# Latent attention: the first pair's queries and keys ahead of the last chunk of the gates' group

## What is computed

```python
def mla_attention(c_q, c_kv, k_rope, q_a_g, kv_a_g, w_q_b, w_kv_b, cos, sin):
    q = (rmsnorm(c_q, q_a_g) @ w_q_b).reshape(b, s, MLA_HEADS, MLA_QK_DIM)
    q_nope = q[..., :MLA_NOPE_DIM]
    q_rope = rope(q[..., MLA_NOPE_DIM:], cos[:, None, :], sin[:, None, :])
    kv = (rmsnorm(c_kv, kv_a_g) @ w_kv_b).reshape(b, s, MLA_HEADS, MLA_NOPE_DIM + MLA_V_DIM)
    k_nope = kv[..., :MLA_NOPE_DIM]
    v = kv[..., MLA_NOPE_DIM:]
    k_r = rope(k_rope, cos, sin)
    ...
        sc = (jnp.einsum('bqhd,bkhd->bhqk', qn, k_nope)
              + jnp.einsum('bqhd,bkd->bhqk', qr, k_r)).astype(jnp.float32) * scale
        ...
        p = jax.nn.softmax(jnp.where(mask, sc, NEG), axis=-1)
        return jnp.einsum('bhqk,bkhd->bqhd', p.astype(v.dtype), v)
...
        proj = h @ w_in[l]
        qa, ka, va, ga, cq, ckv, kr, gb = jnp.split(proj, SPLIT_POINTS, axis=-1)
        ...
        x = x + jnp.concatenate([ya, yb], axis=-1) @ w_out[l]
```

## Time and profile before

| what | value |
|---|---|
| median of 3 runs | 2791.2 us (2790.09 to 2793.32) |
| profiled execution, its time | 2790.87 us |
| its span, first to last instruction | 2789.1 us |
| PE busy | 2732.7 us, 98% |
| DVE, ACT, POOL busy | 45%, 36%, 39% |
| PE idle before a product, for DVE L1443 | 9.9 us in 4 waits, longest 4.0 |

### The profile page before, as it was taken

The page is one execution under the profiler, slowest core; times in us unless marked ns, Lnnn a source line. Parts: engine busy times, 40 slices in busy tenths (PEclk is TensorE's granted clock), DMA queues, the critical chain, the costliest instruction groups (busy, mean ns, idle before and its releaser), DMA issues.

```text
span 2789.1 us, 33326 instructions
## 1 busy us (share of the span) xinstructions
PE 2732.7 (98%) x13100; PEld 2271.2 (81%) x13100; DVE 1241.8 (45%) x1831; ACT 1000.0 (36%) x1566; POOL 1089.6 (39%) x544
## 2 busy tenths in 40 slices
PE   8999998999999999899999999999999999999997
PEld 7888887888888888788878888888878888888886
DVE  6466636622346663672335545553443222222223
ACT  5244435523223443553433333332223323332222
POOL 1443332344443433334443333334344444444442
PEclk9999999999999999999999999999999999999998
DMA  6432231254443223124442232222223333336333
GB/s 183 132 84 76 73 121 45 66 142 143 123 132 91 69 76 121 45 67 138 138 120 76 76 83 76 73 80 80 87 83 121 113 109 111 114 113 211 117 125 113
DMA packets 307611, 289.13 MB, mean 104 GB/s; under 512 B 33152, under 2 KB 256000, under 8 KB 306944
## 3 DMA queue, kind: packets, MB, share of 16 engines
q1 hardware_dynamic: 300512, 264.40, 32.0%
q10 hardware_dynamic: 6944, 22.61, 2.1%
HBM read 260.19 MB, written 26.74 MB: 103 GB/s over the span
## 4 chain that ended last, share of the span: by engine, by line
PE 84%; DVE 11%; DMA 2%; ACT 1%; issue 1%; POOL 0%; SPq 0%; DVEq 0%; ACTq 0%
PE bank L873 25%; PE bank L875 24%; PE bank L874 24%; PE work L1131 1%; DMA w_raw<-in_w_in 1%; DVE pt L1728 1%; PE o_bank L874 1%; PE o_bank L875 1%; DVE mixed L1475 1%; PE work L987 1%; PE work L989 1%; PE o_bank L873 1%; DMA latent_scr<-mixed 1%; DVE probs L1680 1%; DVE mixed L1471 1%
## 5 line engine op out<-in xcount | busy, mean ns | idle before, releaser
L850 POOL TENSOR_TENSOR w_lo<-w_raw,w_hi 128x1024 fp32r<-128x1024 f32 (+3 forms) x460 | 982.0, 2137 | 1367.5 <-ACT w_hi L699 1367.5
L873 PE MATMUL bank<-act_in,w_hi 128*128 128x512 f32 x2662 | 1054.0, 396 | 12.8 <-DVE act_in L1443 9.9
L875 PE MATMUL bank<-act_in,w_lo 128*128 128x512 f32 x2662 | 1041.0, 391 | 0.0
L874 PE MATMUL bank<-act_in,w_hi 128*128 128x512 f32 x2662 | 1039.7, 391 | 0.0
L699 ACT ACTIVATE w_hi<-w_raw 128x1024 fp32r<-128x1024 f32 (+3 forms) x468 | 438.0, 937 | 1049.3 <-PE bank L875 648.4
L873 PEld LDWEIGHTS bank<-act_in,w_hi 128*128 128x128 f32 x2662 | 501.0, 188 | 116.8 <-DVE act_in L1443 11.2
L875 PEld LDWEIGHTS bank<-act_in,w_lo 128*128 128x128 f32 x2662 | 500.5, 188 | 107.2
L874 PEld LDWEIGHTS bank<-act_in,w_hi 128*128 128x128 f32 x2662 | 501.2, 188 | 98.9 <-issue 1.7
L873 PE MATMUL bank<-mixed,w_hi 128*128 128x512 f32 x768 | 299.7, 390 | 0.0
L875 PE MATMUL bank<-mixed,w_lo 128*128 128x512 f32 x768 | 299.1, 389 | 0.0
L874 PE MATMUL bank<-mixed,w_hi 128*128 128x512 f32 x768 | 299.0, 389 | 0.0
(11 more groups left out here) (267 smaller groups left out, 2703.7 us busy)
## 6 DMA issues: line engine op xcount, KB each, us to landing
w_raw<-in_w_in SPq DMA_DIRECT2D x512, 128.0 KB, 2.5
w_raw<-in_w_in SPq DMA_DIRECT2D x224, 256.0 KB, 2.9
w_raw<-in_w_out SPq DMA_DIRECT2D x64, 512.0 KB, 3.7
w_raw<-in_w_in SPq DMA_DIRECT2D x32, 512.0 KB, 3.7
w_raw<-in_w_out SPq DMA_DIRECT2D x64, 256.0 KB, 4.6
x_scr<-buf ACTq DMA_DIRECT2D x32, 256.0 KB, 3.2
probs<-x_scr SPq DMA_DIRECT2D x32, 256.0 KB, 5.0
w_raw<-in_w_attn_up SPq DMA_DIRECT2D x32, 256.0 KB, 2.9
```

The source lines that it names most:

```text
L850: nc.gpsimd.tensor_tensor(lo, raw, hi, ALU.subtract).then_inc(lo_ready, 1)
L873: pe.matmul(dst, lhs[0], rhs[0], start=start, stop=False, skip_group_check=skip)
L874: pe.matmul(dst, lhs[0], rhs[1], start=False, stop=False, skip_group_check=skip)
L875: return pe.matmul(dst, lhs[1], rhs[0], start=False, stop=stop, skip_group_check=skip)
```

## The change

The first pair's `mla0` group is cut in two. Its queries, rotary queries and keys (`mla0` 0, tiles 0 to 2) are made between chunk 6 and chunk 7 of `gb` 1, in the three `work` banks, which are named `bank4` to `bank6` for this. The values (a new group `mlav`) follow behind `gb` 1. Head 0's scores stand right behind `gb` 1 now and ahead of the values, its maxima and exponentials with them; its `mla_norm`, transposes and values are placed relative to `mlav`. The key weights are a chunk of their own (128 columns) and the value weights another (256). The gaps of the four parts of `gb` 1's gates are new, and ACT waits before the first rotary copy until the gates of `gb` 0 are out of `probs2` (`gates_kept`). The number of products is the same; there is one chunk more in each layer.

```diff
-        for i in range(2):
-            group("gb", l, i, full, ["g0", "g1", "g2", "g3"])
+        group("gb", l, 0, full, ["g0", "g1", "g2", "g3"])
+
+        group("mla0", l, 0, [], ["qn", "qr both", "kn"], banks=(4, 5, 6))
+        group("gb", l, 1, full, ["g0", "g1", "g2", "g3"])
         for h in range(0, MLA_HEADS, 2):
-            group("mla0", l, h // 2, [], ["qn", "qr both", "kn", "v both, half the tokens", "v, other half"],
-                  banks=(0, 1, 2, 3, 0))
+            if h == 0:
+                group("mlav", l, 0, [], ["v both, half the tokens", "v, other half"], banks=(None, None, None, 0, 1))
+            else:
+                group("mla0", l, h // 2, [], ["qn", "qr both", "kn", "v both, half the tokens", "v, other half"],
+                      banks=(0, 1, 2, 3, 0))
             group("mla1", l, h // 2, [], ["qn", "kn"], banks=(2, 3))
...
+        if kind == "mlav":
+            head("mla", l, 0, 0, [(2, "mla_norm"), (6, "transpose"), (9, "values"), (12, "output")])
+            steps.append(("mla_scores", len(heads) - 1))
             a = chunk(n, "kv_b", [0, 1])
-            for m in others:
+            for m in (3, 4):
                 product(n, a, m, True, True)
...
             for c, kts in enumerate(g["chunks"]):
+                if kind == "gb" and i == 1 and c == 7:
+                    latent_products(n - 1, (0, 1), (2,))
...
                 if kind == "gb" and i == 1:
-                    at = ((4, 7, 9), (11, 13, 15), (22, 28, 30), (32, 38, 40))[k]
+                    at = ((1, 3, 5), (6, 8, 10), (16, 20, 22), (25, 30, 32))[k]
                 for gap, name in zip(at, ("gate_log", "gate_min", "gate_mul")):
...
+        bank += work
...
                     if g["kind"] == "mla0" and m == 1:
+                        if g["i"] == 0:
+                            act.wait_ge(gates_kept, g["l"] + 1)
...
+                if first and kind == "mla0" and i == 0:
+                    pe.wait_ge(pt_lo, heads[first_mla[l]]["turn0"])
```

More of the change, by code:

```diff
@@ L60 @@
 SB_COLS = 1344
-EARLY_READS = {"mla0": range(5), "mla1": range(2), "swa": (0,), "sb": (0, 1, 2)}
+EARLY_READS = {"mla0": range(5), "mlav": (3, 4), "mla1": range(2), "swa": (0,), "sb": (0, 1, 2)}
 def plan_groups():
@@ L123, in product @@
         if last and m in EARLY_READS.get(kind, ()):
-            if kind in ("mla0", "mla1"):
+            if kind in ("mla0", "mlav", "mla1"):
                 if m < 3:
@@ L128, in product @@
                     later(5 - m, "hi", n, m)
-            lag = {1: 1, 3: 3, 4: 2}.get(m) if kind == "mla0" else None
+            lag = {1: 1, 3: 3, 4: 2}.get(m) if kind in ("mla0", "mlav") else None
             if lag is None:
@@ L163, in plan_steps, with latent_products @@
     later(57, "sum_meta")
+    def latent_products(n, queries, others):
+        a = chunk(n, "q_b", [0, 1])
+        for m in queries:
+            product(n, a, m, True, False)
+        a = chunk(n, "q_b", [2])
+        for m in queries:
+            product(n, a, m, False, True)
+        a = chunk(n, "kv_b", [0, 1])
+        for m in others:
+            product(n, a, m, True, True)
     for n, g in enumerate(groups):
         kind, l, i = g["kind"], g["l"], g["i"]
+        if kind == "mla0" and i == 0:
+            continue
         if kind == "cq" or (kind == "sb" and i == 0):
@@ L170, in plan_steps @@
                 later(18, "spread_x", l, 1)
-        if kind in ("mla0", "mla1"):
-            queries, others = {"mla0": ((0, 1), (2, 3, 4)), "mla1": ((0,), (1,))}[kind]
-            a = chunk(n, "q_b", [0, 1])
-            for m in queries:
-                product(n, a, m, True, False)
-            a = chunk(n, "q_b", [2])
-            for m in queries:
-                product(n, a, m, False, True)
+        if kind == "mlav":
+            head("mla", l, 0, 0, [(2, "mla_norm"), (6, "transpose"), (9, "values"), (12, "output")])
+            steps.append(("mla_scores", len(heads) - 1))
             a = chunk(n, "kv_b", [0, 1])
-            for m in others:
+            for m in (3, 4):
                 product(n, a, m, True, True)
+        elif kind == "mla0":
+            latent_products(n, (0, 1), (2, 3, 4))
+        elif kind == "mla1":
+            latent_products(n, (0,), (1,))
         else:
@@ L199, in plan_steps @@
                     steps.append(("pool_mix", a, t))
-        if kind not in ("mla0", "mla1"):
+        if kind not in ("mla0", "mlav", "mla1"):
             steps.append(("evac", n))
@@ L269, in hybrid_program @@
         for m, b in enumerate(g["banks"]):
+            if b is None:
+                continue
             tile_no[gi, m] = n
@@ L298, in hybrid_program @@
         ys += 0 if h["kind"] == "swa" and h["e"] == 0 else 1
+    first_mla = [next(h["j"] for h in heads if h["kind"] == "mla" and h["l"] == l) for l in range(2)]
     first_sb = next(h["j"] for h in heads if h["kind"] == "sb")
@@ L467, in hybrid_program @@
         gate_out = sem("gate_out")
+        gates_kept = sem("gates_kept")
         mla_hi = sem("mla_hi")
@@ L535, in pieces @@
                     return [((0, 128), rows(w, c0 + 256, 128))]
+                if g["kind"] == "mlav":
+                    return [((0, 128), rows(w, c0 + 128, 128)), ((128, 256), rows(w, c0 + 384, 128))]
+                if i == 0:
+                    return [((0, 128), rows(w, c0, 128))]
                 return [((0, 256), rows(w, c0, 256)), ((256, 384), rows(w, c0 + 384, 128))]
@@ L574, in width @@
             what = chunks[c][1]
-            if groups[chunks[c][0]]["kind"] == "mla1":
-                return 128
+            g = groups[chunks[c][0]]
+            if g["kind"] == "mla1" or (what == "kv_b" and g["kind"] == "mla0" and g["i"] == 0):
+                return 128
+            if g["kind"] == "mlav":
+                return 256
             return {"q_b": 256, "kv_b": 384, "pool_w": 256}.get(what, 512)
@@ L948, in product @@
                     start, stop = first and kk == 0, last and kk == len(kts) - 1
-                    if kind == "mla0" and m >= 3:
+                    if kind in ("mla0", "mlav") and m >= 3:
+                        v0 = 128 if kind == "mla0" else 0
                         x = latent(3 + kt)
@@ L1149, in _ @@
                     if kind == "mla":
-                        pe.wait_ge(tile_ready, tile("mla0", l, h["h"] // 2, 4) + 1)
+                        pe.wait_ge(tile_ready, tile("mla0" if h["h"] > 1 else "mlav", l, h["h"] // 2, 4) + 1)
                     if kind == "sb":
@@ L1568, in _ @@
                                 signal(gate_in)
+                            if g["i"] == 0 and n == 1:
+                                signal(gates_kept)
                         elif g["kind"] != "mix":
```

2 lines of the change are left out of this document (1 added, 1 removed).

## The result

The changed kernel takes 2804.06 us (median of 5 runs, 2801.62 to 2806.37), the kernel before 2792.11 on the same chip (5 runs, 2790.09 to 2793.32): a ratio of 1.0043, with an interval of 1.0032 to 1.0054. It is 12 us slower. The forecast was 2791.4, its range ended at 2796. The profiled execution took 2803.07 us, 12.2 more than that of before.

A forecast was written before the change was run, and what follows sets the result against it. PE, busy 98% of the span, was taken as the bound, so only its waits and slow stretches could yield time: 2790.87 - 5.5 (seam) + 6.6 (gates) - 0.6 (head 5's scores) = 2791.4 us, range 2784.5 to 2796.

The forecast's parts named there:

- The latents, `gates_kept`: Latents needed 5.4 us earlier and the wait for the first gates cost nothing; layer 1's 0.97 us wait should go.
- A new wait for weights: Ahead of the gates' last chunk PE waits about 1.1 us for POOL's pass over its weights.
- 0.9 ahead of head 0's scores: Head 0's scores wait 0.9 us for the rotary chain, taken as 8.14 us long, and start at 428.9.
- 3.1 ahead of head 1's keys: PE waits 3.1 us for head 1's key weights, whose rounding queues on ACT behind exponentials, gates and copies.
- To the scores of head 1: Head 0's transposes to head 1's scores take 4.0 to 5.1 us; scores start at 447.8, a gain of 3.95 us.
- The sum itself: 2790.87 - 5.5 + 6.6 - 0.6 = 2791.4 us; waits moved and clock down once, chance 0.45, own range 2789 to 2794.
- falls again, once: Behind the 3.1 us wait the clock drops for one product's worth, costing 1.3 us in each layer (0 to 2.7).
- The gates of parts three and four, 6.6: At heads 3 and 5 of both layers a DVE, ACT, DVE round trip costs 1.65 us each, 6.6 us.
- the 0.6 that did come back: With `gate_mul` out of the way ahead of head 5's scores, PE's 0.32 us wait goes: 0.6 in both layers.
- The earliest case: At head 3 the gates' round trip ends at 492.8 at the earliest, 1.5 us after the old copies' start, 491.41.
- -5.5 at the seam: Gain up to head 1's scores in both layers, clock loss included: 3.95 + 4.15 - 2.6 = 5.5 us.
- 2806 by a late gates' chunk: Slow rival, chance 0.08: the gates' last chunk lands 7.5 us late from memory, some 15 us, 2806.

The follow-up runs named there:

- e3: Changed kernel with head 1's key weights rounded on ACT right behind head 0's exponentials, part one's gaps at (3, 4, 5): 2799.19 us, ratio 1.0029 to the kernel before.
- e5: e3 with parts three and four of the gates back at their old products, as in e1: 2790.01 us, ratio 0.9995 to the kernel before.
- e4: Changed kernel with head 0's transposes two products earlier: 2804.58 us, ratio 1.0042 to the kernel before.
- e7: e6 with head 0's transposes two products earlier: 2797.17 us, ratio 1.0017 to the kernel before.
- e6: e5 with the three steps of part two of the gates six products later: 2799.12 us, ratio 1.0025 to the kernel before.
- e8: Kernel before with part two of the gates six products later, nothing else: 2801.57 us, ratio 1.0034 to the kernel before.
- e1: Changed kernel with parts three and four of the gates back at their old products: 2795.05 us, ratio 1.0008 to the kernel before.
- e2: Kernel before with only parts three and four of the gates at the changed kernel's places: 2801.01 us, ratio 1.0030 to the kernel before.
- e12: e7 with part two's minimum and its product with the gate each one product earlier: 2785.18 us, ratio 0.9975 to the kernel before.
- e15: e12 with head 1's key weights rounded where the changed kernel rounds them, part one at (1, 3, 5): 2787.75 us, ratio 0.9983 to the kernel before.

## Why the prediction was wrong

*The latents, `gates_kept`:* right; no wait of that kind appears, in layer 1 there is none ahead of the first query, and the gates' last chunk did not wait for memory.

*A new wait for weights, 1.1 (1.4 in layer 1):* right, 0.95 and 1.27. (The prediction's own 422.5 less 421.49 is 1.0.)

*0.9 ahead of head 0's scores:* 1.70 and 1.73. The rotary chain was sized at 8.14 us and took 9.26 (420.18 on ACT to the end of DVE's read, 428.75 + 0.69). DVE and then POOL of the changed kernel:

```profile
423.33 1.82 DVE L1292 TENSOR_TENSOR probs<-probs,sin 128x512 f32<-128x512 f32 x1
425.18 1.11 DVE L1293 TENSOR_TENSOR probs<-probs 128x512 f32<-128x512 f32 x1
```

```profile
423.31 1.29 POOL L883 TENSOR_TENSOR w_lo<-w_raw,w_hi 128x512 fp32r<-128x512 f32 x1 [1.17 <-ACT w_hi L730]
424.83 0.91 POOL L883 TENSOR_TENSOR w_lo<-w_raw,w_hi 128x256 fp32r<-128x256 f32 x1 [0.23 <-ACT w_hi L730]
```

Each DVE step ends 0.55 us behind the end of POOL's pass beside it (424.60 and 425.15; 425.74 and 426.29), and is 1.82 and 1.11 long where the same two steps of the next pair's chain (456.98 and 457.71) take 0.69 alone. The Trainium skill (SBUF — State Buffer, "SBUF: two separate sides") gives the rule for it: the pair of ports is held for the whole instruction. The trace agrees: both steps end only behind POOL's passes. I had weighed that rule for `gate_mul` and not for the chain on which my 0.9 rested.

*3.1 ahead of head 1's keys:* right in place and cause, and nearly in size, 2.68 and 2.32 (e3).

*To the scores of head 1, "I take 447.8":* the first step that failed. They start at 449.90. From head 0's transposes (443.93) it is 5.97 us, not 4.0 to 5.1: I took `gate_mul` out of the way and did not see that ACT's copies would stand behind the rounding of the next pair's key and value weights, whose load is late by the very wait that I had just costed. In e5, where that wait is gone, the load is issued 2.0 us earlier, counted from the start of the first queries. e4 and e7 take the copies out from behind the rounding, and the wait ahead of head 1's scores goes from 1.97 to nothing and from 1.93 to 0.54. Together with the clock I counted 2.65 and 2.85 us of gain to here, 5.5 in all; 1.60 and 0.41 were there, 3.5 less.

*The sum itself* failed next, and for more: it ends at head 1's scores and takes whatever is gained there as kept to the end. Head 1's transposes are 11.05 us behind its scores before (462.80 less 451.75), and 12.53 after: ACT and DVE ran the gates and the next pair's rotary chain at the same times as before (the reciprocal behind the chain at 461.22 before, 460.86 after). With the clock behind them, in layer 0 all of the 1.6 us, and 0.7 more, is gone by head 2's scores; in layer 1 the 0.4 and 1.8. That is 4.5 us in the two layers, for which the sum had nothing. e4 (5.30 us of wait at these transposes) shows the hold; e6 shows that part two makes 1.6 us of it, and e8 that it made 0.1 in the old order. That the way leads over ACT's queue is read from the rows, and the constant distance of 15.57 us in three executions fits it; the rotary copies by themselves were not tested.

*The clock "falls again, once":* it did not fall behind the 2.68 us wait on which I put it. It fell in or right behind the windows of the 1.7 us wait in layer 1, of the 2.50 us ones ahead of head 1's transposes, and of the 1.9 us ones at head 6. By the windows that is up to 5.1 us in and behind the seam, where I had 2.6, and up to 3.4 behind head 6, where I had none.

*The gates of parts three and four, 6.6:* right in mechanism and place, mis-sized. The wait grew by 1.53 (0.35 to 1.88), as worked out, and the clock behind it was not in the term; 9.0 us (e1), 8.7 (e2). Four waits of 1.53, up to 3.4 of clock, less the 0.6 that did come back ahead of head 5's scores, give 8.9. (The earliest case is 492.8 less 491.41, 1.4 and not 1.5.)

In sum: forecast -5.5 at the seam, +6.6 and -0.6 behind; measured +2.7 at the seam (e1 against before; by its ratio's interval 0 to 4.7 us), and +9.0. So of the miss of 12.7 us some 8.2 lie at the seam and 3.0 at the gates. The rival that came near in time, 2806 by a late gates' chunk, was not what happened.

## What to carry to other kernels

Work moved forward on the bounding engine gains only as far as the next thing that another engine's queue releases: follow the sum to the point where the old and the new order wait for the same release, here the transposes of the second head. A small step that makes a round trip between two engines (minimum on one, exponential on the other) holds all that is queued behind it on both; one product's difference in its place was worth 12 us here, part of it because the last of its steps then met only the end of another engine's pass over the weights. When a reordering gives nothing, try the few helper steps around it before dropping it, and give the old order the same help as a control: here the order with its helpers set was worth some 7 us, and as first placed cost 12. The control here had part two's place alone.

## What the runs showed of the hardware

The granted clock fell in or right behind windows with waits of 1.7 to 2.5 us in five places of the changed kernel, and stayed full in the window with the 2.68 us wait; e12, with no wait above 2.0 us in these layers, still has 0.85 between 460 and 470. The profiled execution of e15 has waits of 1.73 and 2.44 us, and full clock throughout these layers' latent heads. No run here tells which of the waits will do it. The runs of one kernel differ by as much: those of the kernel before in the session of e12 spread from 2787.75 to 2795.46, and a run of 2789.21 had a mean clock of 0.995, one of 2795.38 one of 0.993; 0.002 of the span is 5.6 us. That alone is more than eight of the fifteen steps tried here, so the differences of single profiled executions are read wait by wait, and their times only beside the medians.

A step of VectorE on 128x512 values with both inputs in SBUF took 0.69 us alone, and 1.82, 1.11, 1.72 and 2.31 us beside passes of GpSimd over weights (423.33 and 425.18 in the changed kernel, 447.37 before, 476.06 in e7).
